# Building the one-hot factors of a gate matrix: the second key's on GpSimd, token by token, and a new split of the first key's between VectorE and ScalarE

## The reference

```python
i1 = jnp.take_along_axis(half_i[:, :, 0], best_c // PEER_TOPK, axis=-1)
i2 = jnp.take_along_axis(half_i[:, :, 1], best_c % PEER_TOPK, axis=-1)
experts = i1 * PEER_KEYS + i2
gate = jax.nn.softmax(best_s, axis=-1)
act = jax.nn.gelu(jnp.einsum('td,thkd->thk', hb, u_table[experts]))
return jnp.einsum('thk,thkd->td', (gate * act).astype(hb.dtype), v_table[experts])
```

## Time and profile before

| | |
|---|---|
| median of 3 runs | 1754.86 us (1754.44 to 1756.94) |
| profiled execution, its own time | 1755.32 us |
| its span | 1753.5 us |
| granted TensorE clock, mean | 0.993 |
| PE busy | 1691.8 us (96%) |
| DVE busy | 1309.0 us (75%) |
| ACT busy | 1071.8 us (61%) |
| POOL busy | 161.9 us (9%), 136 instructions |

### The profile page before, as it was taken

The page is one execution under the profiler, slowest core; times in us unless marked ns, Lnnn a source line. Parts: engine busy times, 40 slices in busy tenths (PEclk is TensorE's granted clock), DMA queues, the critical chain, the costliest instruction groups (busy, mean ns, idle before and its releaser), DMA issues.

```text
span 1753.5 us, 34071 instructions
## 1 busy us (share of the span) xinstructions
PE 1691.8 (96%) x11462; PEld 1518.8 (87%) x11462; DVE 1309.0 (75%) x2642; ACT 1071.8 (61%) x2218; POOL 161.9 (9%) x136
## 2 busy tenths in 40 slices
PE   7998998999999999999999999999899999999998
PEld 1887688989999878888899999999799898999997
DVE  3788787668989798667666666666776777878887
ACT  2545566735666698666555555555558666666665
POOL 0000005501737200000000000000010000010000
PEclk9899999999999999999999999999999999999999
DMA  8534542125455411555555555555364544555553
GB/s 300 184 106 145 183 150 73 54 97 193 161 175 179 144 37 49 191 192 191 192 185 186 191 183 188 184 187 191 114 214 142 180 139 139 181 181 186 186 183 128
DMA packets 77271, 283.33 MB, mean 162 GB/s; under 512 B 8576, under 2 KB 8576, under 8 KB 76928
## 3 DMA queue, kind: packets, MB, share of 16 engines
q1 hardware_dynamic: 77184, 282.19, 48.5%
HBM read 281.11 MB, written 1.05 MB: 161 GB/s over the span
## 4 chain that ended last, share of the span: by engine, by line
PE 78%; DVE 12%; ACT 5%; issue 2%; POOL 1%; DMA 1%; PEld 0%; PEldq 0%; SPq 0%; ACTq 0%; POOLq 0%; DVEq 0%
PE banks L905 20%; PE banks L893 17%; PE banks L984 9%; PE banks L1145 7%; PE banks L496 6%; PE banks L1169 3%; PE banks L835 2%; DVE split L2423 2%; PE banks L461 2%; DVE arena L2419 2%; PE banks L998 1%; PE banks L684 1%; DMA arena<-wstream 1%; PE banks L1105 1%; PE banks L669 1%
## 5 line engine op out<-in xcount | busy, mean ns | idle before, releaser
L1503 ACT ACTIVATE split<-arena 128x512 fp32r<-128x512 f32 x492 | 309.0, 629 | 134.9 <-PE banks L893 76.9
L893 PEld LDWEIGHTS banks<-split 128*128 128x128 f32 x2880 | 355.4, 192 | 10.5 <-DVE split L2349 3.1
L905 PE MATMUL banks<-split 128*128 128x512 f32 x1536 | 361.9, 390 | 1.0 <-issue 1.0
L893 PE MATMUL banks<-split 128*128 128x256 f32 x2880 | 358.8, 283 | 3.1 <-DVE split L2349 2.3
L2441 DVE TENSOR_TENSOR split<-arena,split 128x512 fp32r<-128x512 f32 x396 | 270.5, 690 | 105.4 <-ACT split L1503 99.7
L905 PEld LDWEIGHTS banks<-split 128*128 128x128 f32 x1536 | 283.8, 188 | 57.3 <-issue 1.4
L1481 ACT ACTIVATE split<-arena 128x512 fp32r<-128x512 f32 x312 | 194.5, 628 | 109.9 <-PE banks L1145 52.8
L984 PE MATMUL banks<-split 128*128 128x256 f32 x1728 | 216.6, 286 | 4.3 <-DVE split L2519 3.9
L984 PEld LDWEIGHTS banks<-split 128*128 128x128 f32 x1728 | 211.8, 193 | 7.2 <-issue 6.0
L2496 DVE TENSOR_TENSOR split<-arena,split 128x512 fp32r<-128x512 f32 x180 | 123.0, 695 | 59.5 <-ACT split L1481 57.6
L496 PE MATMUL banks<-split 128*128 128x256 f32 (+1 forms) x912 | 147.1, 320 | 4.3 <-DVE split L1915 3.4
(11 more groups left out here) (425 smaller groups left out, 2342.2 us busy)
## 6 DMA issues: line engine op xcount, KB each, us to landing
arena<-wstream SPq DMA_DIRECT2D x525, 512.0 KB, 3.3
arena<-x_t SPq DMA_DIRECT2D x1, 2048.0 KB, 12.9
arena<-matsa SPq DMA_DIRECT2D x1, 1260.5 KB, 6.2
out_t<-arena SPq DMA_DIRECT2D x4, 256.0 KB, 2.0
arena<-mats SPq DMA_DIRECT2D x1, 576.0 KB, 8.0
arena<-crow SPq DMA_DIRECT2D x1, 512.0 KB, 7.1
arena<-rows SPq DMA_DIRECT2D x1, 512.0 KB, 5.9
arena<-mats SPq DMA_DIRECT2D x1, 449.0 KB, 3.8
```

The costliest lines, as they stand in the source:

```text
L893: mm = pe.matmul(ps[:, 4 + b, 0:S], w_parts[:, c, (2 * m + half) % 4, P * k:P * k + P], h_parts[:, e, 4 * half + k, :], start=(half == 0 a ...
L905: mm = pe.matmul(ps[:, 2 * tt + half, :], g_parts[:, e, j % 2, P * tt:P * tt + P], w_parts[:, c, (2 * m + half) % 4, :], start=(first and ...
L1503: act.activation(w_parts[:, 0, (2 * m + half) % 4, :], ring[:, peer_slot(m), 512 * half:512 * half + 512], ACT.Copy).then_inc(sem["w_hi"], 1)
```

## The change

The one-hots of the second key go to POOL: one `tensor_scalar` with `is_equal` per token, whose second operand is a column of `rT` (a value for each partition), eight per group, with one signal behind the eighth. DVE's instruction for `hot2` is gone. Of `hot1`, DVE makes 6 tokens in the wide `is_equal` (768 elements) and 2, with their gates, by `tensor_scalar`; ACT scales 6. PE takes tokens 6 and 7 first, then 0 to 5.

```diff
@@ TensorE
-                for t in (7, 0, 1, 2, 3, 4, 5, 6):
-                    if t == 7:
-                        pe.wait_ge(sem["hot1_gated"], g + 1)
+                for t in (6, 7, 0, 1, 2, 3, 4, 5):
+                    if t >= 6:
+                        pe.wait_ge(sem["hot1_gated"], 2 * g + t - 5)
                     else:
-                        pe.wait_ge(sem["hot1_scaled"], 7 * g + t + 1)
+                        pe.wait_ge(sem["hot1_scaled"], 6 * g + t + 1)
@@ ScalarE
-                for t in range(7):
+                for t in range(6):
@@ VectorE
-                dve.tensor_tensor(hot1[g % 2][:, 0:7, :], bc(mat("iota"), 1, 7), bc(rT[:, 0, 8 * g:8 * g + 7], 2, P), ALU.is_equal).then_inc(
+                dve.tensor_tensor(hot1[g % 2][:, 0:6, :], bc(mat("iota"), 1, 6), bc(rT[:, 0, 8 * g:8 * g + 6], 2, P), ALU.is_equal).then_inc(
                     sem["hot1_ready"], 1)
                 if g >= 2:
                     w_gate(g - 2)
-                dve.tensor_tensor(hot2[:, g % 2, :, :], bc(mat("iota"), 1, 8), bc(rT[:, 1, 8 * g:8 * g + 8], 2, P), ALU.is_equal).then_inc(
-                    sem["hot2_ready"], 1)
-                t = 8 * g + 7
-                dve.tensor_scalar(hot1[g % 2][:, 7, :], mat("iota"), rT[:, 0, t:t + 1], rT[:, 2, t:t + 1],
-                                  ALU.is_equal, ALU.mult).then_inc(sem["hot1_gated"], 1)
+                for i in (6, 7):
+                    t = 8 * g + i
+                    dve.tensor_scalar(hot1[g % 2][:, i, :], mat("iota"), rT[:, 0, t:t + 1], rT[:, 2, t:t + 1],
+                                      ALU.is_equal, ALU.mult).then_inc(sem["hot1_gated"], 1)
@@ GpSimd, behind its last expert tile
+            pool.wait_ge(sem["phase"], 4 * 3)
+            for g in range(S // 8):
+                if g >= 2:
+                    pool.wait_ge(sem["w_psum"], 8 * g - 8)
+                for i in range(8):
+                    t = 8 * g + i
+                    o = pool.tensor_scalar(hot2[:, g % 2, i, :], mat("iota"), rT[:, 1, t:t + 1], None, ALU.is_equal)
+                o.then_inc(sem["hot2_ready"], 1)
             add_quads(1, sq3, 3 * KT)
```

## The result

The changed kernel takes **1834.76 us** (median of 4 runs, 1833.73 to 1835.88) against 1755.9 us before: ratio 1.0453, 95% interval 1.0437 to 1.0468. That is 79 us slower; 18.8 us were forecast, and the range ended at 1800 us. The mechanism was the forecast one, POOL sets the pace of the gate matrix, but its instruction costs far more than assumed: one starts every 0.579 us instead of every 0.33 us.

The account below looks back on a forecast made before the run. DVE was taken to bound the stage (2.88 us per group), then POOL: 2.64 + 0.71 + 0.14 = 3.49 us, PE's last group at 710.7 instead of 691.89 us, +18.8 us, 1773.7 us; range 1744 to 1800 us.

Parts of the forecast that it names:

- What bounds the stage: Gate-matrix stage before the change: DVE bounds it with 2.88 us per group; at most 10.5 us to be won.
- POOL sets the pace: Changed stage: POOL needs 3.49 us per group, over PE's 2.58 and DVE's 2.88; 18.8 us slower; 52% for 1758 to 1799 us.
- x: Pace of POOL's tensor_scalar of 128 elements for hot2: 0.33 us, 2.64 us per group; bounds 0.17 and 0.43 us.
- For the slope I go near one stream: Per-element part of POOL's instruction, set near one input stream: 0.30 us with 0.16 us fixed, before 0.03 us for the column.
- the upper bound: POOL's 128-element instruction at the two-input price, 0.16 + 0.265 = 0.43 us; 4.29 us per group, 1799 us.
- dearer than a two-input instruction: Rival: POOL's tensor_scalar takes above 0.43 us for fetching its column, more than +44 us; 1817 us at 0.5 us; 10%.
- The hold by DVE: DVE's two-input line 2419 and its tensor_scalars hold POOL off, adding 0.71 + 0.14 us per group.
- DVE waiting for POOL: DVE waits up to x for each of three instructions, 1.88 + 1.0 = 2.9 us per group, still covered by POOL.
- The exclusion costs POOL nothing: Rival: POOL's fixed part runs on while DVE holds the port; 2.64 us per group, 1746 us; 7%.
- The clock: Rival: TensorE's clock falls as PE is busy only 2.58 of 3.49 us; at half clock +73 us, 1828 us; 2%.

Follow-up runs that it names:

- the memset run: Changed kernel, but POOL fills each 128-element row of hot2 with a constant instead of comparing, so it reads nothing: 1745.26 us.
- the multiplication's run: Changed kernel, but POOL's tensor_scalar multiplies iota by the key instead of comparing, with size and column operand kept: 1831.78 us.
- the copy's: Changed kernel, but POOL copies the 128 elements of iota in place of each compare: 1754.85 us.
- the half-of-the-tokens run: Changed kernel, but POOL makes only the last four of eight hot2 tokens and DVE the first four in one wide is_equal: 1778.0 us.
- the two-input run: Changed kernel, but POOL runs eight tensor_tensor subtractions of 128 elements, iota less the repeated key, instead of the compares: 1778.71 us.

## Why the prediction was wrong

**What bounds the stage: right.** DVE's 2.88 us, with 10.5 us to be won at most: the memset run, where hot2 costs nobody anything, won 10. ACT stands closer than its place in the text suggests: DVE's work cut to 2.74 us gave groups of 2.85 us, not 2.74.

**"POOL sets the pace": right.** 256 rows of line 2963 without a gap, PE waiting for them.

**The step that failed is x, "For the slope I go near one stream", and the upper bound ahead of it.** I took the two-input instruction as the dearest that a one-input one could be, 0.43 us. The runs gave 0.579 us = 0.16 fixed (as read) + 0.087 for the column (0.03 assumed) + 128 x 2.59 ns (1.03 to 2.07 assumed). A tensor_scalar takes more per element than a tensor_tensor, and a copy far less. The number of inputs, from which I drew the line, orders them wrongly. Even the row that I leaned on did not give 0.30 us: less the fixed part it gives 0.37 us, which is what two inputs with one repeated cost (0.358), and the way from there down to one stream was an assumption. 32 x 8 x (0.579 - 0.33) = 64 us: all of the error of 61 us and a little more. The rival "dearer than a two-input instruction" had named the outcome, with 10%, and its sum at 0.5 us stood at 1817 us; it should have had more, as no row showed this operation on this engine. Its reason, the fetch of the column, is only the smaller part: with a constant the instruction costs 0.492 us, already above 0.43. Why GpSimd's tensor_scalar takes 2.59 ns per element is open; the multiplication's run rules out the compare, and the copy's the output type and the single input.

**The hold by DVE: right in kind, 0.65 instead of 0.85 us.** 5.28 - 8 x 0.579 = 0.65 us per group. One instruction in eight is 0.60 us longer (0.71 assumed), the one behind it, beside the tensor_scalars, 0.07 us (0.14 assumed); these two are medians over the groups. With x = 0.579 the prediction's sum would have been 8 x 0.579 + 0.85 = 5.48 us per group, the last at 774.4 us, 1837 us.

**DVE waiting for POOL: wrong, though it changed nothing.** I had up to x for each of three instructions. Line 2419 has a median of 959 ns in the changed kernel, its length beside memsets too, while POOL's instruction was always in flight, and the tensor_scalars have 339 ns.

**"The exclusion costs POOL nothing": refuted** by the rows of 1.2 us beside line 2419, by the half-of-the-tokens run, where the sum with the holds comes out within 0.07 us, and by the two-input run, whose groups are 0.72 us longer than 8 x 0.358 us.

**The clock: it fell, at another pace than the rival had it, and without a price.** The rival had it fall in groups of 3.49 us. In the two-input run, with groups of 3.59 us, full clock was granted from 615 to 710 us; with the constant and groups of 4.49 us it was 0.95 from 615 to 740 us. In the changed kernel, from 615 to 770 us 0.86 of full speed was granted, between the two levels, so part of the time at the lower one (windows of the changed kernel, busy of PE, PEld, DVE, ACT, POOL, then PEclk):

```profile
615.00:770.00 155.00, 102.91 (x570) 88.36 (x570) 58.30 (x120) 75.13 (x204) 154.73 (x235) 0.86 0.06 21
```

A group of products takes 2.05 us or, like the one after a gap of 2.90 us, 3.00 us:

```profile
701.44 2.05 PE L947 MATMUL banks<-split,arena 128*128 128x128 f32 x16 [2.47 <-POOL split L2963]
703.33 0.60 PE L930 MATMUL banks<-arena 128*128 128x256 f32 x2
706.82 3.00 PE L947 MATMUL banks<-split,arena 128*128 128x128 f32 x16 [2.90 <-POOL split L2963]
```

It costs nothing, since POOL is not kept waiting by it: its groups stay between 5.1 and 5.5 us behind the first.

## What to carry to other kernels

An operation that no row shows on the engine it is moved to needs its own measurement before anything is worked out from it; the rows of another operation there did not bound it from above, though that one had more inputs. Where two engines hold each other off, add the holds to the work of the one that never rests, and look for the place of moved work beside instructions that read PSUM, where nothing was held here. Lightening the engine that sets the pace helps only down to the next one, here ACT. And read first what the stage can give at all: here 10 us, against eight small instructions a group whose price was unknown.

## What the runs showed of the hardware

- GpSimd, 128 partitions x 128 elements, start to start: fill 0.147 us, copy 0.238 us, tensor_tensor 0.358 us, tensor_scalar with a constant 0.492 us, with a column 0.579 us, whether it compares or multiplies. The Trainium skill ("GPSIMD Engine Reference", section on engine selection) calls one-input work roughly line-rate; the 0.27 us estimated from that in the prediction comes near the copy and not the tensor_scalar, and the measurement decides.
- DVE's two-input instruction of 768 elements lengthens a GpSimd instruction by 0.60 us, while GpSimd's tensor_scalars of 128 elements did not lengthen that DVE row (median 959 ns). Those of 64 elements did, to a median of 1080 ns, and GpSimd's two-input tensor_tensors of 128 elements to 1184 ns. Against those of 512 or 1024 elements DVE waits long, up to 1.95 us for a tensor_scalar of 0.34 us. The Trainium skill ("SBUF — State Buffer", summary of rules for kernel authors) has the second to issue blocked until the first is done. The long ones agree, and so does the GpSimd instruction that starts behind line 2419; that line, starting while a GpSimd tensor_scalar of 128 elements is in flight, does not wait for it. Why was not tried.
- A fill on GpSimd reads nothing and is not lengthened beside the same DVE rows: longest 207 ns. But fills without a gap held DVE's tensor_scalars of 0.34 us for up to 1.68 us, and line 2419 beside fills kept its 959 ns.
